# Adding expert outputs to the residual stream inside the scatter DMA instead of in a combine stage (mixer, attention and two top-2 expert layers, one Trainium2 core)

## The chip, the cores and the metric

The kernel runs on one core of a Trainium2 chip. Its metric is the device time of one execution in microseconds (us). Names used below: PE is TensorE (matrix products), DVE is VectorE, ACT is ScalarE, POOL is GpSimd, SP is SyncE, which here only issues DMAs.

## The reference

A two-layer trunk over 1040 positions (16 meta tokens and 1024 inputs) of width 1024, in fp32. Layer 0 is a state-space mixer, layer 1 windowed attention; each is followed by a mixture of experts. The part that the change touches is the end of the expert layer:

```python
def run_block(args):
    xblk, e = args
    hid = jax.nn.silu(xblk @ w_gate[e]) * (xblk @ w_up[e])
    return hid @ w_down[e]

yb = lax.map(run_block, (xb, blk_e)).reshape(n_rows, D)
contrib = yb[dest] * sgate[:, None].astype(yb.dtype)
out = jnp.zeros_like(t).at[stok].add(contrib)
...
h = h + hier_moe(rmsnorm(h, norm_ffn[layer]), ...)
```

Every token goes to two of 32 experts (`N_EXPERTS` 32, `TOP_K` 2), and the two outputs are weighted by two gates and added to the residual h. At the end of the trunk stands a last RMSNorm.

## The kernel before

The kernel has four stages one after the other: the mixer, expert layer 0 (`phase_moe(nc, t, 0)`), attention, expert layer 1 (`phase_moe(nc, t, 1, out)`). The residual h lies in SBUF the whole time, as 9 tiles of 128 tokens (the ninth has the 16 meta tokens). The order of the work on each engine is written out by hand, with semaphores between the engines.

**An expert layer.** First the router: h is normalized tile by tile, the normalized rows are stored to `xn_dram` by SP, the logits, the gates and a sorted list of rows are made. The list says for each work tile (128 slots, one expert) which token's row stands in each slot; slots beyond an expert's rows hold an index out of bounds, and the DMA leaves them out. Then comes a loop over work tiles, 32 in each layer here (64 in both). In an iteration:

- SP loads the expert's three matrices as six pieces of 1 MB into six buffers `raw` (lines 1340 to 1350). A buffer is loaded again as soon as DVE has made the low part of its old content.
- ACT casts each piece to fp32r (`hi`, line 1533), DVE subtracts to make `lo` (line 1763), PE multiplies (lines 1930 to 1932, three products for each pair of operands). `hi` and `lo` have three slots each.
- POOL gathers the 128 rows of a later work tile from `xn_dram` into `xg` (`gather`, line 1459).
- ACT copies the 128x1024 result from PSUM to `y` (`store_y`, line 1553), and POOL scatters `y` to `y_dram` (`scatter`, line 1465). `y_dram` has two rows for each token, one for each of its two experts. POOL then waits for that scatter to land before it raises `y_free`, for which the next `store_y` waits.

The order on POOL in the loop is: gather for tile e+2, wait for `y_done(e)`, scatter of tile e-1, wait for its landing:

```python
with pool.Fori(1, n_q - 2) as e:
    pool.wait_ge(xt_mm, e + 2)
    column(gi, idx_in, e + 2, e * 2 + 1)
    gather(gi[:, :])
    pool.wait_ge(y_done, e)
    scatter(e - 1, e * 2 + 2)
```

`column` copies one column of an index table and is followed by a small multiplication (lines 1450 and 1453). On ACT the eviction stands at the end of an iteration: `hi` pieces 6e+3, 6e+4, 6e+5, the cast of x, `hi` pieces of the next tile, the cast of the hidden rows, `store_y(e - 1)`. The next instruction is the `hi` cast of piece 3 of the next iteration.

**The combine.** When all scatters have landed, `y_dram` is read back, 1 MB for each tile of 128 tokens (two rows of 4 KB for each token), and DVE adds the two rows, each times its gate, to h with two `scalar_tensor_tensor` (line 1058 in layer 0, in `combine`; line 1837 in layer 1). In layer 0 (`projections`) the norm of h, its transposes and the K, V and Q products follow tile by tile, on ACT (squares, line 1028; normalize, line 1039; hi part, line 1032), DVE (line 1065) and PE (lines 1121 and 1139). In layer 1 follow squares on ACT (line 1603), two small operations on POOL (lines 1492 and 1493) that make the reciprocal root, the final scaling on DVE (line 1830) and the store to `out`.

## Time and profile before

| | |
|---|---|
| median of 3 runs | 2108.0 us (2107.89 to 2123.16) |
| time of the profiled execution | 2108.43 us |
| its span, first to last instruction | 2106.3 us |
| PE busy | 1920.0 us (91%) |
| DVE busy | 1582.0 us (75%) |
| ACT busy | 1251.5 us (59%) |
| POOL busy | 381.9 us (18%) |

"Busy" counts an instruction's own duration; waits are idle time. The profiled execution's time lies 2.1 us above its span, so sums on the span can be carried over to the time by adding that. More than half of the span is the two loops over experts, from about 450 to 1018 and from about 1484 to 2050 us.

### The profile page before, as it was taken

What the parts mean: (1) busy time and instruction counts of PE and PEld (TensorE: products, weight loads), DVE (VectorE), ACT (ScalarE), POOL (GpSimd) and SP (SyncE); (2) the same over time, 40 slices, a digit from 0 to 9 for tenths busy, and PEclk for the clock granted to TensorE, in tenths of its full rate; (3) what the DMA queues carried; (4) which work ended last, traced back from release to release, by engine and by line L of the source; (5) the groups of instructions that cost most, each with busy time, mean ns of one, the idle gap of its engine ahead of it and who ended that gap; (6) DMA issues with size and microseconds to landing.
All of it is one profiled execution on the core that took longest, in us unless ns stands there. A gap on an engine that the chain in (4) does not pass through costs nothing. (4 is left out here: it accounts for less than half of the span.)

```text
span 2106.3 us, 31639 instructions
## 1 busy us (share of the span) xinstructions
PE 1920.0 (91%) x10610; PEld 1576.8 (75%) x10610; DVE 1582.0 (75%) x1774; ACT 1251.5 (59%) x1538; POOL 381.9 (18%) x674
## 2 busy tenths in 40 slices
PE   4949999869999999999699999996999999999991
PEld 3638777758888888888598777775788888888880
DVE  8997321479999999999752376656799999999985
ACT  6615210437887777777530165544577777787771
POOL 2000000312222122221233000002122223211224
PEclk9979999989999999999899999998999999999995
DMA  4174300449999999999612110006599999999976
GB/s 105 25 76 145 110 1 1 184 153 377 385 386 378 378 381 381 385 390 389 249 61 71 35 58 2 1 1 262 205 368 364 382 383 388 398 395 395 388 300 250
DMA packets 136174, 504.72 MB, mean 240 GB/s; under 512 B 38610, under 2 KB 68626, under 8 KB 84882
## 3 DMA queue, kind: packets, MB, share of 16 engines
q1 hardware_dynamic: 114786, 468.72, 60.3%
q0 software_dynamic: 18432, 33.86, 4.2%
q10 hardware_dynamic: 2880, 1.12, 0.4%
q8 instruction: 48, 0.79, 0.2%
q14 instruction: 28, 0.23, 0.0%
HBM read 488.47 MB, written 47.32 MB: 254 GB/s over the span
## 5 line engine op out<-in xcount | busy, mean ns | idle before, releaser
L1763 DVE TENSOR_TENSOR moe_lo<-moe_raw,moe_hi 128x2048 fp32r<-128x2048 f32 x378 | 861.2, 2292 | 89.5 <-ACT moe_hi L1533 84.4
L1533 ACT CAST moe_hi<-moe_raw 128x2048 fp32r<-128x2048 f32 x374 | 712.0, 1915 | 127.1 <-PE moe_ps_g L1932 59.1
L1930 PE MATMUL moe_ps_y<-moe_hi,moe_h_hi 128*128 128x512 f32 x512 | 205.5, 401 | 3.8 <-DVE moe_h_lo L1779 3.8
L1930 PE MATMUL moe_ps_g<-moe_hi,moe_x_hi 128*128 128x512 f32 x512 | 205.9, 402 | 1.9 <-DVE moe_x_lo L1787 1.9
L1932 PE MATMUL moe_ps_y<-moe_lo,moe_h_hi 128*128 128x512 f32 x512 | 200.8, 392 | 0.0
L1931 PE MATMUL moe_ps_y<-moe_hi,moe_h_lo 128*128 128x512 f32 x512 | 200.5, 392 | 0.0
L1932 PE MATMUL moe_ps_g<-moe_lo,moe_x_hi 128*128 128x512 f32 x512 | 199.9, 390 | 0.0
L1932 PE MATMUL moe_ps_u<-moe_lo,moe_x_hi 128*128 128x512 f32 x512 | 199.7, 390 | 0.0
L1931 PE MATMUL moe_ps_g<-moe_hi,moe_x_lo 128*128 128x512 f32 x512 | 199.5, 390 | 0.0
L1930 PE MATMUL moe_ps_u<-moe_hi,moe_x_hi 128*128 128x512 f32 x512 | 199.4, 389 | 0.0
L1931 PE MATMUL moe_ps_u<-moe_hi,moe_x_lo 128*128 128x512 f32 x512 | 199.2, 389 | 0.0
L1540 ACT CAST moe_x_hi<-moe_ps_xt 128x1024 fp32r<-128x1024 f32 x60 | 61.0, 1017 | 101.3 <-PE moe_ps_xt L1915 101.3
L1930 PEld LDWEIGHTS moe_ps_y<-moe_hi,moe_h_hi 128*128 128x128 f32 x512 | 96.8, 189 | 22.5 <-DVE moe_lo L1763 4.2
L1930 PEld LDWEIGHTS moe_ps_g<-moe_hi,moe_x_hi 128*128 128x128 f32 x512 | 97.0, 189 | 20.7 <-DVE moe_x_lo L1787 2.3
L1932 PEld LDWEIGHTS moe_ps_y<-moe_lo,moe_h_hi 128*128 128x128 f32 x512 | 96.5, 189 | 20.7
L1932 PEld LDWEIGHTS moe_ps_g<-moe_lo,moe_x_hi 128*128 128x128 f32 x512 | 96.1, 188 | 21.2
L1932 PEld LDWEIGHTS moe_ps_u<-moe_lo,moe_x_hi 128*128 128x128 f32 x512 | 96.1, 188 | 20.0
L1930 PEld LDWEIGHTS moe_ps_u<-moe_hi,moe_x_hi 128*128 128x128 f32 x512 | 96.1, 188 | 19.9
L1931 PEld LDWEIGHTS moe_ps_u<-moe_hi,moe_x_lo 128*128 128x128 f32 x512 | 96.1, 188 | 19.9
L1931 PEld LDWEIGHTS moe_ps_y<-moe_hi,moe_h_lo 128*128 128x128 f32 x512 | 96.6, 189 | 18.5
L1931 PEld LDWEIGHTS moe_ps_g<-moe_hi,moe_x_lo 128*128 128x128 f32 x512 | 96.4, 188 | 18.0
L1450 POOL COPY moe_si<-moe_idx_out 128x1 int32 x64 | 50.3, 786 | 327.2 <-ACT moe_y L1553 327.2
(503 smaller groups left out, 3711.9 us busy)
## 6 DMA issues: line engine op xcount, KB each, us to landing
moe_raw<-moe_w_gate SPq DMA_DIRECT2D x128, 1024.0 KB, 8.7
moe_raw<-moe_w_up SPq DMA_DIRECT2D x128, 1024.0 KB, 9.1
moe_raw<-moe_w_down SPq DMA_DIRECT2D x128, 1024.0 KB, 8.7
mix_r<-ssm_w_glu SPq DMA_DIRECT2D x16, 512.0 KB, 6.0
xn_dram<-moe_work SPq DMA_DIRECT2D x16, 512.0 KB, 8.8
prj_yc<-y_dram SPq DMA_DIRECT2D x8, 1024.0 KB, 7.0
moe_raw<-y_dram SPq DMA_DIRECT2D x8, 1024.0 KB, 11.6
mix_r<-x SPq DMA_DIRECT2D x8, 512.0 KB, 5.1
```

The lines of the kernel that those rows point to most:

```text
L1450: G_.tensor_copy(dst[:, :], idx[:, bass.ds(tile, 1)]).then_inc(ix_step, 1)
L1533: A.copy(hi[:, slot(number, k), :], raw[:, k, :]).then_inc(hi_done, 1)
L1540: A.copy(x_hi[:, :, :].rearrange("p c m -> p (c m)"), ps_xt[:, :]).then_inc(xt_hi, 1)
L1763: V.tensor_tensor(lo[:, slot, :], raw[:, k, :], hi[:, slot, :].bitcast(F32), ALU.subtract).then_inc(lo_done, 1)
L1930: T.matmul(out, x_h, w_h, start=first, stop=False)
L1931: T.matmul(out, x_l, w_h, start=False, stop=False)
L1932: return T.matmul(out, x_h, w_l, start=False, stop=final)
```

## The change

- h is copied to DRAM (`acc_dram0`, `acc_dram1`) before the expert loop: six tiles already at the end of the stage before (mixer, attention), the others after the router's stores. These stores are issued by SP.
- The gates are stored to `gate_dram` by SP after the router, and DVE makes a table `idx_gate` that says for each slot of each work tile where its gate lies. `y_dram` and `idx_out` are gone.
- For each work tile POOL gathers 128 gates of 4 bytes from `gate_dram` into `gate` (`gather_gate`). ACT's eviction waits for that gather and multiplies by the gate on the way (`activation` with `scale=gate`).
- The scatter goes to the token's row of `acc_dram` and adds (`compute_op=ALU.add`) instead of writing to a row of its own.
- The combine is gone: after the last scatter SP loads h back, 512 KB for each tile. ACT's squares wait for the load of their tile.

```diff
+STORED = XT - 2
...
             sp.dma_start(t["gain"][:, :], t["norm_ffn"][0].partition_broadcast(P)).then_inc(gain_in, 16)
+            for i in range(STORED):
+                sp.wait_ge(h_done, (NQ - 1) * NT + i + 1)
+                sp.dma_start(t["acc_dram0"][i * P:(i + 1) * P, :], h[:, i, :]).then_inc(acc_out, 16)
             sp.wait_ge(gain_in, 16)
+            sp.wait_ge(acc_out, 16 * STORED)
...
     def project_sp(sp):
         for j in range(NT):
             i, n = TILE_ORDER[j], tile_rows(TILE_ORDER[j])
-            if j >= N_YC:
-                sp.wait_ge(h_new, 2 * (j - N_YC + 1))
-            sp.dma_start(yc[0:n, j % N_YC], y_pairs[2 * i * P:2 * (i * P + n), :].rearrange("(p k) d -> p k d", k=2)
-                         ).then_inc(yc_in[j % N_YC], 16)
+            sp.dma_start(h[0:n, i, :], t["acc_dram0"][i * P:i * P + n, :]).then_inc(h_in[j], 16)
...
         for j in range(NT):
-            combine(j)
             if j >= 2:
                 lo_part(j - 2)
...
+            for i in range(STORED, NT):
+                sp.dma_start(acc_dram[i * P:i * P + rows(i), :], h[0:rows(i), i, :]).then_inc(acc_in, 16)
             for k in range(4):
+                if k == 3:
+                    sp.wait_ge(gates_done, 1)
+                    sp.dma_start(gate_dram.rearrange("(p k) o -> p (k o)", p=P),
+                                 gates[:, :, :].rearrange("p k i -> p (k i)")).then_inc(gates_out, 16)
                 sp.wait_ge(lo_done, first_pieces(k) + 1)
                 load(k, 1)
...
             for i in range(NT if last_layer else 0):
-                if i >= NB:
-                    sp.wait_ge(h_new, 2 * (i - NB + 1))
-                sp.dma_start(yc[0:rows(i), i % NB],
-                             y_dram[2 * i * P:2 * (i * P + rows(i)), :].rearrange("(p k) d -> p k d", k=2)
-                             ).then_inc(yc_in[i % NB], 16)
+                sp.dma_start(h[:, i, :], acc_dram[i * P:(i + 1) * P, :]).then_inc(h_in[i], 16)
...
             def scatter(tile, step):
-                column(si, idx_out, tile, step)
-                G_.indirect_dma_start(y_dram[:, :], bass.IndirectOffsetOnAxis(si[:, :].bitcast(U32), 0),
-                                      y[:, :], None,
-                                      bounds_check=last_y, oob_is_err=False).then_inc(y_out, 16)
+                column(si, idx_in, tile, step)
+                G_.indirect_dma_start(acc_dram[:, :], bass.IndirectOffsetOnAxis(si[:, :].bitcast(U32), 0),
+                                      y[:, :], None, bounds_check=last_row, oob_is_err=False,
+                                      compute_op=ALU.add).then_inc(y_out, 16)
                 pool.wait_ge(y_out, tile * 16 + 16)
                 G_.tensor_tensor(unit[:, 1:2], mhalf[:, :], mhalf[:, :], ALU.mult).then_inc(y_free, 1)
+
+            def gather_gate(tile, step):
+                column(hi_gate, idx_gate, tile, step)
+                G_.indirect_dma_start(gate[:, :], None, gate_dram[:, :],
+                                      bass.IndirectOffsetOnAxis(hi_gate[:, :].bitcast(U32), 0),
+                                      bounds_check=last_gate, oob_is_err=False).then_inc(gate_in, 16)
...
+            pool.wait_ge(gate_at, 1)
+            pool.wait_ge(gates_out, 16)
+            gather_gate(0, 3)
+            pool.wait_ge(acc_in, 16 * (NT - STORED))
             with pool.Fori(1, n_q - 2) as e:
                 pool.wait_ge(xt_mm, e + 2)
-                column(gi, idx_in, e + 2, e * 2 + 1)
+                column(gi, idx_in, e + 2, e * 3 + 1)
                 gather(gi[:, :])
                 pool.wait_ge(y_done, e)
-                scatter(e - 1, e * 2 + 2)
+                scatter(e - 1, e * 3 + 2)
+                gather_gate(e, e * 3 + 3)
...
             def store_y(e, used):
                 act.wait_ge(w_used, used)
                 act.wait_ge(y_free, e + 1)
-                A.copy(y[:, :], ps_y[:, :]).then_inc(y_done, 1)
+                act.wait_ge(gate_in, e * 16 + 16)
+                A.activation(y[:, :], ps_y[:, :], ACT.Copy, scale=gate[:, 0:1]).then_inc(y_done, 1)
```

How the change moves instructions, at the two places that matter most. The first is POOL in the loop over work tiles. Before, from the copy of the scatter's index column (`moe_si`) to the end of the iteration:

```order
L1450 COPY moe_si<-moe_idx_out 128x1
L1451 REGISTER_ALU
L1453 TENSOR_TENSOR moe_unit<-moe_mhalf 128x1
L1465 DMA y_dram<-moe_y,moe_si 2080x1024
L1468 ISA
L1469 TENSOR_TENSOR moe_unit<-moe_mhalf 128x1
```

After, from the same copy on (`moe_gate` takes the gathered gates, `moe_hi_gate` the index column for them):

```order
L1449 COPY moe_si<-moe_idx_in 128x1
L1450 REGISTER_ALU
L1452 TENSOR_TENSOR moe_unit<-moe_mhalf 128x1
L1464 DMA acc_dram<-moe_y,moe_si 1040x1024
L1467 ISA
L1468 TENSOR_TENSOR moe_unit<-moe_mhalf 128x1
L1449 ISA
L1449 COPY moe_hi_gate<-moe_idx_gate 128x1
L1450 REGISTER_ALU
L1452 TENSOR_TENSOR moe_unit<-moe_mhalf 128x1
L1472 DMA moe_gate<-gate_dram,moe_hi_gate 128x1
```

The gate's gather stands behind the wait for the scatter's landing (line 1467 after, 1468 before), and ahead of the next iteration's gather of x.

The second is DVE at the end of layer 1. Before:

```order
L1779 TENSOR_TENSOR moe_h_lo<-moe_ps_ht,moe_h_hi 128x512
L1837 SCALAR_TENSOR_TENSOR h<-moe_raw,moe_gates,h 128x1024 x6
L1830 SCALAR_TENSOR_TENSOR h<-h,moe_rstd,gain 128x1024
L1837 SCALAR_TENSOR_TENSOR h<-moe_raw,moe_gates,h 128x1024 x2
L1830 SCALAR_TENSOR_TENSOR h<-h,moe_rstd,gain 128x1024
```

After:

```order
L1797 TENSOR_TENSOR moe_h_lo<-moe_ps_ht,moe_h_hi 128x512
L1848 SCALAR_TENSOR_TENSOR h<-h,moe_rstd,gain 128x1024 x8
```

The 16 additions of the combine are gone, and the 8 final scalings stand alone.

## Rows read from the trace of the kernel before

**Rows 1.** Stretches: start:end us, length, busy us (x instructions) by engine, PE clock, DMA share, GB/s.

```profile
700.00:800.00 100.00, 100.00 (x475) 83.88 (x474) 90.11 (x50) 79.12 (x58) 20.13 (x38) 1.00 0.99 380
...
2080.00:2107.00 27.00, 0.00 (x0) 0.00 (x0) 20.12 (x16) 5.75 (x10) 15.04 (x12) 0.50 0.63 249
```

**Rows 2.** Timeline of ACT, one iteration: start, us, line, operation.

```profile
1839.50 1.01 ACT L1553 COPY moe_y<-moe_ps_y 128x1024 f32<-128x1024 f32 x1
1840.43 1.92 ACT L1533 CAST moe_hi<-moe_raw 128x2048 fp32r<-128x2048 f32 x1
...
1857.24 1.02 ACT L1553 COPY moe_y<-moe_ps_y 128x1024 f32<-128x1024 f32 x1
```

**Rows 3.** Timeline of POOL, the same iteration; [idle before <-releaser].

```profile
1841.92 1.02 POOL L1465 DMA_INDIRECT y_dram<-moe_y,moe_si  x1 [0.15 <-issue]
1850.32 0.18 POOL L1469 TENSOR_TENSOR moe_unit<-moe_mhalf 128x1 f32<-128x1 f32 x1 [7.38 <-DMA y_dram<-moe_y,moe_si]
...
1851.54 1.06 POOL L1459 DMA_INDIRECT moe_xg<-xn_dram,moe_gi  x1 [0.31 <-issue]
```

**Rows 4.** Line 1465 (scatter), then line 1459 (gather): us from issue to landing.

```profile
DMA to landing us min/median/max: 3.2/8.8/9.7
...
DMA to landing us min/median/max: 3.3/8.1/11.6
```

**Rows 5.** DMA of 1520 to 1580; last number: median us to landing.

```profile
DMA packets 3816, 22.15 MB, mean 369 GB/s; under 512 B 1034, under 2 KB 1034, under 8 KB 1194
...
q0 software_dynamic: 873, 0.66, 3.3%
...
y_dram<-moe_y,moe_si POOLq DMA_INDIRECT x4, 8.6
moe_xg<-xn_dram,moe_gi POOLq DMA_INDIRECT x3, 5.7
```

**Rows 6.** The same of 1880 to 1940, where the tiles have more rows.

```profile
DMA packets 3935, 23.87 MB, mean 398 GB/s; under 512 B 707, under 2 KB 707, under 8 KB 1337
...
q0 software_dynamic: 1008, 2.58, 10.8%
...
moe_xg<-xn_dram,moe_gi POOLq DMA_INDIRECT x3, 7.6
y_dram<-moe_y,moe_si POOLq DMA_INDIRECT x3, 8.8
```

**Rows 7.** Timelines of DVE and PE: a `lo` piece, and the first product after it.

```profile
1842.38 2.29 DVE L1763 TENSOR_TENSOR moe_lo<-moe_raw,moe_hi 128x2048 fp32r<-128x2048 f32 x1 [0.34 <-ACT moe_hi L1533]
...
1845.67 0.39 PE L1930 MATMUL moe_ps_u<-moe_hi,moe_x_hi 128*128 128x512 f32 x1
```

**Rows 8.** The chain that ended last, at the end of layer 1: start, us, what.

```profile
2064.52 5.04 DMA moe_raw<-y_dram
...
2097.93 1.30 POOL moe_ss L1492
...
2099.27 0.60 POOLq L1186
2099.89 1.28 DVE h L1830
```

**Rows 9.** Timelines after layer 0: ACT's first squares; PE's transposes of two tiles.

```profile
1037.26 1.06 ACT L1028 ACTIVATE gain<-h 16x1024 f32<-16x1024 f32 x1 [10.51 <-DVE h L1058]
...
1062.22 1.16 PE L1121 MATMUL moe_ps_y<-moe_ident,prj_xn 128*128 128x128 f32 x8
...
1066.32 1.16 PE L1121 MATMUL moe_ps_xt<-moe_ident,prj_xn 128*128 128x128 f32 x8
```

**Rows 10.** Timelines of ACT and POOL at the last tile of layer 0, then of layer 1.

```profile
1025.74 1.01 ACT L1553 COPY moe_y<-moe_ps_y 128x1024 f32<-128x1024 f32 x1 [1.32 <-POOL moe_unit L1469]
...
2055.49 0.18 POOL L1469 TENSOR_TENSOR moe_unit<-moe_mhalf 128x1 f32<-128x1 f32 x1 [2.26 <-DMA y_dram<-moe_y,moe_si]
...
2059.09 1.01 ACT L1553 COPY moe_y<-moe_ps_y 128x1024 f32<-128x1024 f32 x1 [7.79 <-PE moe_ps_y L1932]
```

More of the change, by code:

```diff
@@ L1052, in project_dve @@
         V = nc.vector
-        def combine(j):
-            i, n = TILE_ORDER[j], tile_rows(TILE_ORDER[j])
-            dve.wait_ge(yc_in[j % N_YC], 16 * (j // N_YC + 1))
-            for k in range(2):
-                V.scalar_tensor_tensor(h[0:n, i, :], yc[0:n, j % N_YC, k, :], gates[0:n, k, i:i + 1],
-                                       h[0:n, i, :], ALU.mult, ALU.add).then_inc(h_new, 1)
-                dve.wait_ge(h_new, 2 * j + k + 1)
         def lo_part(j):
@@ L1181, in phase_moe @@
     h = t["h"]
-    xn_dram, y_dram = t[f"xn_dram{layer}"], t[f"y_dram{layer}"]
+    xn_dram, acc_dram, gate_dram = t[f"xn_dram{layer}"], t[f"acc_dram{layer}"], t[f"gate_dram{layer}"]
     w_gate = t["moe_w_gate"][layer].rearrange("e (p c) f -> e p c f", c=DC)
@@ L1252, in phase_moe @@
         si = sb("si", [P, 1], I32)
+        hi_gate = sb("hi_gate", [P, 1], I32)
+        gate = sb("gate", [P, 1])
         lead(nc, sb, t["qkv_at"])
@@ L1599, in _ @@
                 for i in range(NT):
[L1600 removed]
+                    act.wait_ge(h_in[i], 16)
                     if i:
@@ L1742, in _ @@
             V.scalar_tensor_tensor(idx_in[:, :], table, float(NO_ROW), row[:, :], ALU.add, ALU.min).then_inc(rows_ready, 1)
[L1743 to L1745 removed]
             link(V.tensor_tensor(after[0:1, :, :], incl[0:1, :].unsqueeze(1).to_broadcast([1, XTR, N_EXP]),
                                  iota_t[0:1, 0:XTR].unsqueeze(2).to_broadcast([1, XTR, N_EXP]), ALU.is_le))
[L1748 to L1749 removed]
+            link(V.reduce_sum(more[0:1, :], after[0:1, :, :], AX.X))
+            V.tensor_copy(tile_exp[0:1, N_EXP:TILES], more[0:1, :]).then_inc(list_ready, 1)
             V.tensor_copy(n_more[0:1, :], incl[0:1, N_EXP - 1:N_EXP]).then_inc(list_ready, 1)
@@ L1754, in _ @@
             link(V.tensor_tensor(gates[:, 0, :], col["pg"][:, :], col["tmpc"][:, :], ALU.mult))
-            link(V.tensor_tensor(gates[:, 1, :], gates[:, 0, :], col["e2"][:, :], ALU.mult))
+            V.tensor_tensor(gates[:, 1, :], gates[:, 0, :], col["e2"][:, :], ALU.mult).then_inc(gates_done, 1)
+            dve.wait_ge(rows_ready, 1)
+            V.tensor_scalar(second[:, :], table, 0.0, None, ALU.is_lt)
+            V.tensor_single_scalar(at_i[:, 0, :], idx_in[:, :], P - 1, ALU.bitwise_and)
+            link(V.tensor_single_scalar(at_i[:, 1, :], idx_in[:, :], 7, ALU.logical_shift_right))
+            link(V.tensor_copy(at[:, :, :], at_i[:, :, :]))
+            link(V.scalar_tensor_tensor(at[:, 0, :], at[:, 0, :], 2.0 * NT, at[:, 1, :], ALU.mult, ALU.add))
+            V.scalar_tensor_tensor(idx_gate[:, :], second[:, :], float(NT), at[:, 0, :], ALU.mult, ALU.add).then_inc(gate_at, 1)
             dve.wait_ge(list_ready, 2)
@@ L1833, in _ @@
             for i in range(NT if last_layer else 0):
-                n = rows(i)
-                dve.wait_ge(yc_in[i % NB], 16 * (i // NB + 1))
-                for k in range(2):
-                    V.scalar_tensor_tensor(h[0:n, i, :], yc[0:n, i % NB, k, :], gates[0:n, k, i:i + 1],
-                                           h[0:n, i, :], ALU.mult, ALU.add).then_inc(h_new, 1)
-                    dve.wait_ge(h_new, 2 * i + k + 1)
-                if last_layer and i >= 2:
-                    final_scale(i - 2)
-            if last_layer:
-                for i in range(NT - 2, NT):
-                    final_scale(i)
+                final_scale(i)
         @block.tensor
```

55 lines of the change are left out of this document (28 added, 27 removed).

## The prediction

> **What bounds the kernel now.** I read the stretches first. In a stretch inside a loop over experts PE is busy for the whole 100 us at the full clock, and the DMA engines at a share of 0.99 and 380 GB/s, while in the last 27 us PE does nothing and DVE is busy for 20.12 [rows 1]. So there are two kinds of time: two loops whose period PE sets, and two ends where the combine and the norm run. Next comes one iteration on the timelines. `store_y` starts at 1839.50 and again at 1857.24, so the period is 17.74 us [rows 2]. The waits in this stretch are short on every engine but POOL, which sits through the landing of its scatter. What counts for the change is not how busy POOL is but how its steps stand in a ring: `store_y` starts, 2.42 us later the scatter is issued (1841.92), it lands and POOL goes on at 1850.32, and the DMA after it is issued 1.22 us later, at 1851.54 [rows 2, 3]. Today this ring closes early: `y_free` comes at 1850.5 and is wanted at 1857.24. Last, the chain of waits at the end of layer 1 goes through the load of `y_dram`, DVE, POOL and DVE again to 2101.17, with 5.1 us of storing after it [rows 8].
>
> **What the ends give back.** Layer 1: the reload starts at 2064.52 in both kernels. Before, the first 1 MB took 5.04 us [rows 8]; the first 512 KB should take about 3.6 (between the 3.2 of a scatter on idle engines [rows 4] and that 5.04), so to 2068.1. Squares 1.25, then the two POOL operations and the first final scaling: about 2071.6. After that the eight tiles follow each other as POOL and DVE let them. In the trace a POOL operation beside a running DVE one takes 1.30, and the second one 0.60 with DVE idle, then DVE takes 1.28 [rows 8]. The first of the two hides under DVE's scaling of the tile before it, so a tile costs 1.28 + 0.60 + some 0.1 of handing over, 2.0. Seven more tiles end at 2085.6, and with the same 5.1 us of storing the span ends at 2090.7: 15.6 us less. That the out stores and the reload would bound it instead is unlikely: 8.4 MB in some 25 us is below the rate of the loops.
>
> Layer 0: two `scalar_tensor_tensor` go from each tile, but PE's transposes of two successive tiles stand 4.10 us apart (1062.22 and 1066.32, [rows 9]) with products of about 2.9 us and transposes of 1.2 us between, so PE takes the place of DVE as the limit. Only the front is shorter: ACT's first squares start at 1037.26, and would start at the landing of a small load, near 1034.4. I take 2.9 us. The ends together give 18.5.
>
> **What the ends lose.** The last `store_y` of a layer now waits for a gate gather that is issued 1.22 us after the scatter before it has landed, and takes at least the 3.3 us of the fastest gather [rows 4]. In layer 0 that scatter had just landed when `store_y` started at 1025.74, so it starts near 1029.9: 4.2 us. In layer 1: 2055.49 + 1.22 + 3.3 = 2060.0 in place of 2059.09, 0.9 us [rows 10]. The last two scatters of each layer also become read-and-add; priced below at 1.1 us each, 4.4 for four. So the ends net 18.5 - 5.1 - 4.4 = 9.0 us.
>
> **The loop, where the sum is decided.** Three things are new for each work tile: the scatter adds, a gather of 128 gates is issued behind the wait for the scatter's landing, and `store_y` waits for it. The ring is then: `store_y` to scatter issue 2.42, scatter landing S, its adding A, 1.22 to the gate gather's issue, its landing G, and 0.13 that I allow for an eviction that scales (the plain one takes 1.01, [rows 2]). If the ring is longer than 17.74, it is the period, whatever slack the other buffers have. S + A + G may be 17.74 - 2.42 - 1.22 - 0.13 = 13.97 us at most.
> S: the median is 8.8 [rows 4]. It hardly depends on rows: in 1520 to 1580 the software queue has 873 packets and 0.66 MB, that is 6 DMAs of about 27 rows, and a scatter lands after 8.6; in 1880 to 1940 it has 1008 packets and 2.58 MB, 7 DMAs of about 90 rows, and a scatter lands after 8.8 [rows 5, 6]. So what it costs is 128 small steps beside a queue that always has weights in it. I take 8.7.
> G: no row shows a gather of 4 bytes for each partition. From below 3.3, a gather on idle engines; from above 8.1, the median of the gathers of x [rows 4]. The nearest rows are the three gathers of about 27 rows, which leave out 101 of their 128: 5.7 [rows 5]. They also stand in the very slot where the gate gather will stand. I take 5.7.
> A: not shown either. From below 0. Between 27 and 90 rows a scatter grows by 0.2 and a gather by 1.9 [rows 5, 6]; reading 65 rows more lies between these, and I take 1.1. From above a whole further trip like a gather's, 5.7.
> Ring: 2.42 + 8.7 + 1.1 + 1.22 + 5.7 + 0.13 = 19.27, 1.53 more than now. Is that consistent? An iteration moves 6 loads of 1.05 MB, 65 rows each way and 65 more for the adding, 7.1 MB; in 19.27 us that is 368 GB/s, the load under which 5.7 and 8.6 were measured (369, [rows 5]). There are 29 such steps in each loop, so 58 x 1.53 = 88.7. The first delay of each loop is taken by slack: the `lo` piece that comes next after `store_y` on ACT and DVE ends at 1844.67 and is wanted at 1845.67 [rows 7], 1.0 us, twice: 86.7.
>
> Behind the waiting `store_y` on ACT is queued the `hi` cast of the next piece, which starts the moment the eviction ends, at 1840.43 [rows 2]; DVE waits for that, and PE for DVE. So beyond the 1.0 us the wait reaches PE in full. On POOL the gather of x for a later tile is pushed back by the gate gather, by about 2 us plus A. Issued at 1851.54 and landing 8.1 later [rows 3, 4], it is wanted by the transposes of the period after, so I take it as hidden.
>
> What the Trainium skill says of this, "DMA: Bandwidth & Descriptors", section "Anatomy of one DMA — SWDGE (gpsimd) path": a software DMA costs about 2.0 us fixed plus its bytes at 436 GB/s, so 512 bytes of gates would take 2.0, the ring would be about 15.5 and nothing would stall. The trace speaks against it in the loop (5.7 with 27 rows), and no row reaches 2.0 even idle (3.2). Of the adding, "Collectives: The Full Stack", section "The bandwidth ceiling: the fold count and why AG ≠ RS ≠ AR", says that a reduction costs twice a copy because each element has two source reads; taken for this, A would be a gather's 1.9 rather than 1.1, and the time 46 us higher. No run here shows it yet.
>
> **Edits at nothing.** The copies of h to `acc_dram`: 4.2 MB in each layer, issued while PE is in long products of the stage before, and for the last tiles behind the router's stores; their cover gone, 1 MB at 398 GB/s [rows 6] is 2.6 us in each layer. The gate table: six small DVE operations, some 1.3 us, in the time in which the first x gather is in flight; three others, 0.6 us, go from the path to the list. The gate store: 9 to 18 numbers for each partition behind loads that nobody waits for.
>
> **Sum.** 2108.4 (the profiled execution, 0.4 above the median) - 9.0 + 86.7 = 2186 us.
>
> **Rivals.**
> (1) The ring fits: G + A is at most 13.97 - 8.7 = 5.3 us, for instance G at the idle 3.3 and A up to 2.0. Then the loops keep their 17.74 us and the ends alone count: 2108.4 - 18.5 + 5.1 + 0 to 4.4, that is 2095 to 2099. For it: the gates are 512 bytes, and a 4-byte piece may pass faster than even a skipped row. Against it: landing hardly depends on bytes in [rows 5, 6]. This is the one that ends on the other side, not slower; it decides at G + A = 5.3, and up to 5.5 it would still be within 1%. To be over 1% faster it needs ends that give some 8 us more than I find.
> (2) The DMA engines become the bound rather than the ring: G is short but their share is 0.99 to 1.00 already at 380 GB/s [rows 1]. 0.27 MB more in each iteration at that rate is 0.7 us, 60 iterations: 42, less 9: 2141. Against it: 398 GB/s are moved with PE as fast as ever in [rows 6].
> (3) Adding is much dearer, A of 3 or more: ring over 21.2, 2290 and more.
>
> **How the numbers follow.** Forecast, a ring of 18.5 to 20.8: 0.53. Rival 1: 0.27, of which 0.10 over 1% faster and 0.17 within 1%. Rival 2 and short rings of 17.9 to 18.5: 0.13, of which 0.06 within 1%. Rival 3: 0.07. About 1% is what a measurement of this kernel can tell from no change. Range 2093 to 2270: from rival 1's lower end to a ring of 20.75 (G 6.6, A 1.7); it leaves out the better half of the fast cases and rival 3. Faster by over 1% 0.10, within 1% 0.24, slower 0.66.
>
> **What would show it.** In the profile after: starts of `store_y` 19.3 us apart; ACT idle before `store_y` with the gate DMA as releaser, 1 to 2 us in each iteration; PE idle before a product of `ps_u` with DVE's `lo` as releaser; gate gathers landing after 5 to 6 us, scatters after 9.8; from the last scatter's landing to the end of the span 26 us rather than 42. Wrong if `store_y` waits for nothing in the loop, or if PE's waits are on `raw` loads (then rival 2).

## The result and the profile after

The changed kernel took 2359.1 us (median of 4 runs, 2356.58 to 2361.62) against 2108.8 for the kernel before on the same chip: ratio 1.1165, 95% interval 1.1128 to 1.1202. It is 250 us slower, above the range of the prediction (2093 to 2270).

The first view is a table of stretches of the changed kernel: start:end and length in us, then busy us (number of instructions) of PE, PE's weight loads, DVE, ACT and POOL, then PE's granted clock (1.00 is 2.4 GHz, 0.50 is 1.2 GHz), the DMA share and GB/s. The first row is the stretch of [rows 1]; the others are one iteration, cut up.

```profile
700.00:800.00 100.00, 86.38 (x393) 71.49 (x393) 73.21 (x42) 64.67 (x47) 38.30 (x47) 0.93 0.87 307
...
817.00:825.00 8.00, 5.87 (x26) 4.51 (x25) 2.07 (x2) 0.29 (x1) 4.05 (x5) 1.00 0.95 365
825.00:829.00 4.00, 0.00 (x0) 0.00 (x0) 1.35 (x1) 4.00 (x3) 1.99 (x3) 0.70 0.11 35
829.00:833.00 4.00, 3.01 (x7) 2.43 (x8) 4.00 (x3) 2.70 (x3) 0.00 (x0) 0.50 0.73 155
833.00:838.00 5.00, 5.00 (x26) 4.24 (x26) 2.76 (x3) 2.46 (x2) 4.04 (x7) 0.96 0.98 336
```

PE no longer fills the loop: 86 of 100 us, with holes in which the DMA engines fall idle too (share 0.11). So neither of them is the bound. The costliest groups on the page say who waits (busy us, mean ns | idle before, releaser):

```profile
L1938 PE MATMUL moe_ps_u<-moe_hi,moe_x_hi 128*128 128x512 f32 x512 | 225.3, 440 | 195.3 <-DVE moe_lo L1781 195.3
...
L1468 POOL TENSOR_TENSOR moe_unit<-moe_mhalf 128x1 f32<-128x1 f32 x64 | 77.2, 1206 | 432.3 <-DMA acc_dram<-moe_y,moe_si 432.3
...
L1566 ACT ACTIVATE moe_y<-moe_ps_y,moe_gate 128x1024 f32<-128x1024 f32 x64 | 71.5, 1117 | 241.4 <-DMA moe_gate<-gate_dram,moe_hi_gate 241.4
```

`store_y` (line 1566) waits 241.4 us for the gate gather, in 33 of 64 tiles and not in each one, and PE loses 195.3 us of it before the products of `ps_u`. Line 1468, a product of 128 single numbers, takes 1206 ns on average; such an operation takes 0.18 alone [rows 3]. The timeline of ACT has two kinds of iteration:

```profile
798.78 1.12 ACT L1566 ACTIVATE moe_y<-moe_ps_y,moe_gate 128x1024 f32<-128x1024 f32 x1
...
824.71 1.11 ACT L1566 ACTIVATE moe_y<-moe_ps_y,moe_gate 128x1024 f32<-128x1024 f32 x1 [8.08 <-DMA moe_gate<-gate_dram,moe_hi_gate]
...
843.29 1.12 ACT L1566 ACTIVATE moe_y<-moe_ps_y,moe_gate 128x1024 f32<-128x1024 f32 x1
```

One step of 25.9 us, then one of 18.6; over 58 steps of both loops (the first 29 of each) the mean is 22.15 against 17.75 before, and 28 of them are longer than 22. 58 x 4.40 is 255 us, and the spans differ by 252.9: the loops hold the whole loss, and all else together gives back about 2 us. The timeline of POOL in the long step shows where its 25.9 us go:

```profile
801.19 1.64 POOL L1464 DMA_INDIRECT acc_dram<-moe_y,moe_si  x1 [0.15 <-issue]
812.19 1.78 POOL L1468 TENSOR_TENSOR moe_unit<-moe_mhalf 128x1 f32<-128x1 f32 x1 [9.36 <-DMA acc_dram<-moe_y,moe_si]
813.91 2.25 POOL L1449 COPY moe_hi_gate<-moe_idx_gate 128x1 int32 x1
816.24 2.29 POOL L1452 TENSOR_TENSOR moe_unit<-moe_mhalf 128x1 f32<-128x1 f32 x1
818.67 1.09 POOL L1472 DMA_INDIRECT moe_gate<-gate_dram,moe_hi_gate  x1
...
833.19 1.21 POOL L1468 TENSOR_TENSOR moe_unit<-moe_mhalf 128x1 f32<-128x1 f32 x1 [4.78 <-DMA acc_dram<-moe_y,moe_si]
```

2.4 to the scatter's issue, 11.0 to POOL's next operation, 6.5 from there to the gate gather's issue, 6.0 to `store_y`. The 6.5 us are three tiny operations, which end at 813.97, 816.16 and 818.53. DVE's timeline has this beside them:

```profile
811.62 6.85 DVE L1781 TENSOR_TENSOR moe_lo<-moe_raw,moe_hi 128x2048 fp32r<-128x2048 f32 x3
```

Three subtractions without a gap, ending near 813.9, 816.2 and 818.4: each POOL operation ends when a subtraction ends. The Trainium skill, "SBUF — State Buffer", section "Who interferes with whom", says that a DVE instruction with two SBUF inputs contends with a GpSimd instruction that reads SBUF, and the page's section "Summary: rules for kernel authors" that the second of the two to issue fully blocks until the first finishes. The `lo` subtraction has two (`raw` and `hi`), and the trace agrees, at 2.25 and 2.29 us for operations that take 0.2 alone. The rest of this trace says the same: 153 small POOL operations begin while a `lo` subtraction runs, and take 1.71 us in the median and up to 2.31; 51 begin while DVE runs one of its subtractions or products with one input in PSUM (`x_lo`, `h_lo`, `hid`), and take 0.18 to 0.20.

Before the change, the same run of three subtractions stands at the same phase, and POOL is done just ahead of it (timelines of POOL and DVE, kernel before; `store_y` had started at 611.55):

```profile
622.84 0.19 POOL L1469 TENSOR_TENSOR moe_unit<-moe_mhalf 128x1 f32<-128x1 f32 x1 [7.84 <-DMA y_dram<-moe_y,moe_si]
623.29 0.18 POOL L1450 COPY moe_gi<-moe_idx_in 128x1 int32 x1 [0.27 <-issue]
623.56 0.19 POOL L1453 TENSOR_TENSOR moe_unit<-moe_mhalf 128x1 f32<-128x1 f32 x1
```
```profile
624.39 6.86 DVE L1763 TENSOR_TENSOR moe_lo<-moe_raw,moe_hi 128x2048 fp32r<-128x2048 f32 x3
```

The run lies from 12.8 to 19.7 us after `store_y`. A landing at 11.3 gets its three operations through in 0.9 us. A landing at 13.4 does not get the gate gather out before the run is over, at 19.9. That is a step, not a slope. The kernel before came to this edge once: in the step whose `store_y` starts at 1732.98 the landing comes 12.2 us after it, the run starts at 1745.81, and the third of POOL's operations and the issue behind it are held up (POOL's timeline; the x gather goes out 3.2 us after the landing instead of 1.2):

```profile
1745.86 2.29 POOL L1453 TENSOR_TENSOR moe_unit<-moe_mhalf 128x1 f32<-128x1 f32 x1
1748.30 2.93 POOL L1459 DMA_INDIRECT moe_xg<-xn_dram,moe_gi  x1
```

Last, the stall costs PE's clock. Its timeline around the hole, with the first product after it at twice the usual length:

```profile
829.99 0.80 PE L1938 MATMUL moe_ps_u<-moe_hi,moe_x_hi 128*128 128x512 f32 x1 [7.12 <-DVE moe_lo L1781]
...
833.15 0.53 PE L1939 MATMUL moe_ps_u<-moe_hi,moe_x_lo 128*128 128x512 f32 x1
833.52 0.40 PE L1940 MATMUL moe_ps_u<-moe_lo,moe_x_hi 128*128 128x512 f32 x1
```

After 7.1 us of idleness PE runs at 1.2 GHz until about 833.2. The eight products that start from 829.99 on take 3.5 us to pass instead of 1.8, so 1.7 us more. The pair of steps adds up: 25.9 + 18.6 - 2 x 17.74 = 9.0, of which 7.1 is idleness and 1.7 the clock.

### The profile page after: what moved, and what is told of

Same layout as the page of the kernel before. It is cut to its first block and busy times, and to the rows that moved or that the text cites. A ratio compares the mean times of both kernels' runs of the same rounds, so it can differ in the third digit from the quotient of the medians.

```text
span 2359.2 us, 31996 instructions
## 1 busy us (share of the span) xinstructions
PE 1983.7 (84%) x10610; PEld 1615.3 (68%) x10610; DVE 1535.8 (65%) x1746; ACT 1251.3 (53%) x1538; POOL 671.2 (28%) x866
## 5 line engine op out<-in xcount | busy, mean ns | idle before, releaser
L1938 PE MATMUL moe_ps_u<-moe_hi,moe_x_hi 128*128 128x512 f32 x512 | 225.3, 440 | 195.3 <-DVE moe_lo L1781 195.3
L1938 PEld LDWEIGHTS moe_ps_u<-moe_hi,moe_x_hi 128*128 128x128 f32 x512 | 108.5, 212 | 230.0 <-DVE moe_lo L1781 207.1
L1939 PE MATMUL moe_ps_u<-moe_hi,moe_x_lo 128*128 128x512 f32 x512 | 218.2, 426 | 0.0
L1940 PE MATMUL moe_ps_u<-moe_lo,moe_x_hi 128*128 128x512 f32 x512 | 216.3, 423 | 0.0
L1468 POOL TENSOR_TENSOR moe_unit<-moe_mhalf 128x1 f32<-128x1 f32 x64 | 77.2, 1206 | 432.3 <-DMA acc_dram<-moe_y,moe_si 432.3
L1566 ACT ACTIVATE moe_y<-moe_ps_y,moe_gate 128x1024 f32<-128x1024 f32 x64 | 71.5, 1117 | 241.4 <-DMA moe_gate<-gate_dram,moe_hi_gate 241.4
L1786 DVE TENSOR_TENSOR moe_x_lo<-moe_ps_xt,moe_x_hi 128x1024 fp32r<-128x1024 f32 x60 | 73.5, 1224 | 81.6 <-ACT moe_x_hi L1552 81.6
L1449 POOL COPY moe_si<-moe_idx_in 128x1 int32 x64 | 27.3, 427 | 346.2 <-ACT moe_y L1566 346.1
L1939 PEld LDWEIGHTS moe_ps_u<-moe_hi,moe_x_lo 128*128 128x128 f32 x512 | 109.0, 213 | 22.6
L1464 POOL DMA_INDIRECT acc_dram<-moe_y,moe_si x64 | 107.2, 1674 | 15.4 <-issue 15.4
```

What stands on the lines that cost most here:

```text
L1449: G_.tensor_copy(dst[:, :], idx[:, bass.ds(tile, 1)]).then_inc(ix_step, 1)
L1464: G_.indirect_dma_start(acc_dram[:, :], bass.IndirectOffsetOnAxis(si[:, :].bitcast(U32), 0), y[:, :], None, bounds_check=last_row, oob_is_ ...
L1468: G_.tensor_tensor(unit[:, 1:2], mhalf[:, :], mhalf[:, :], ALU.mult).then_inc(y_free, 1)
L1566: A.activation(y[:, :], ps_y[:, :], ACT.Copy, scale=gate[:, 0:1]).then_inc(y_done, 1)
L1786: V.tensor_tensor(x_lo[:, :, :].rearrange("p c m -> p (c m)"), ps_xt[:, :], x_hi[:, :, :].bitcast(F32).rearrange("p c m -> p (c m)"), ALU. ...
L1938: T.matmul(out, x_h, w_h, start=first, stop=False)
```

## The experiments

The first four kernels ran together on one chip (before: 2110.0 us), the next four together (2108.7), the next three (2110.7), the last by itself (2109.9). `landed` below is the second half of `scatter`: the wait for `y_out` and the operation that raises `y_free`. The times after `store_y` that follow are differences of start times in the timelines of ACT and POOL.

**1. Gate gather first** (`e1_gate_first`). Two calls change places, with their step numbers:

```diff
-                scatter(e - 1, e * 3 + 2)
-                gather_gate(e, e * 3 + 3)
+                gather_gate(e, e * 3 + 2)
+                scatter(e - 1, e * 3 + 3)
```

> Only the order on POOL changes: the gather of the gates for tile e is issued before the scatter of tile e-1 instead of behind its landing, so gather and scatter run side by side. Theory (the ring store_y, scatter landing, gate gather, store_y sets the period of 22.2 us): the ring is then 2.4 + some 2 for issuing the gates + 6.4 to 11 for the scatter, under 17.74, PE sets the period again and the 4.5 us on each of 60 steps go: 2359 - 267, about 2092, a little under the kernel before. Rival A (the added DMA work, 0.27 MB of reading and 144 small packets for each tile, fills the DMA engines and sets the period): waits on the weight loads appear and the time stays above 2150. Rival B (scatter 11 us and more under full load, with 2 us of gate issue ahead of it, is itself too long): ACT waits for POOL's y_free, and the time is 2100 to 2130.

Measured: 2251.4 us (ratio 1.067, 1.065 to 1.069). The gate waits are gone and 108 us with them, but 141 remain. The wait is the one that rival B named, ACT for `y_free`, but rival B had 2100 to 2130 us. POOL's timeline shows the ring:

```profile
799.06 1.05 POOL L1472 DMA_INDIRECT moe_gate<-gate_dram,moe_hi_gate  x1
800.12 1.65 POOL L1449 COPY moe_si<-moe_idx_in 128x1 int32 x1
801.86 2.13 POOL L1452 TENSOR_TENSOR moe_unit<-moe_mhalf 128x1 f32<-128x1 f32 x1
804.14 3.50 POOL L1464 DMA_INDIRECT acc_dram<-moe_y,moe_si  x1 [0.15 <-issue]
815.52 1.58 POOL L1468 TENSOR_TENSOR moe_unit<-moe_mhalf 128x1 f32<-128x1 f32 x1 [7.88 <-DMA acc_dram<-moe_y,moe_si]
```

What stood ahead of the scatter put it among the next subtractions of DVE: issued 7.6 us after `store_y` instead of 2.4, landed some 18 to 21 after it, and `store_y` waits for `y_free` (166.2 us in all, 59 times), every 20.4 us. The issue of the scatter itself is stretched, 3.50 us against 1.63.

**2. No gates** (`e2_no_gate`). Leaves out the gates.

```diff
-                gather_gate(e, e * 3 + 3)
...
-                act.wait_ge(gate_in, e * 16 + 16)
-                A.activation(y[:, :], ps_y[:, :], ACT.Copy, scale=gate[:, 0:1]).then_inc(y_done, 1)
+                A.copy(y[:, :], ps_y[:, :]).then_inc(y_done, 1)
```

> The gather of gates is left out and the eviction is the plain copy, so the output lacks the gates; the adding scatter stays. Theory (ring through the gate gather): without its last link the ring is 2.4 + 11 at most, and the loops go back to 17.74 us a tile: 2090 to 2100. Rival A (the adding scatter's DMA work sets the period): above 2130, with waits on the loads.

Measured: 2203.9 us (1.044, 1.041 to 1.047). The expectation fell, and with it the theory that the gate ring is all. The waits of 600 to 1000 (us in total, times, longest) name another ring:

```profile
POOL moe_unit L1468 <- DMA acc_dram<-moe_y,moe_si: 188.4, 21, 10.0
...
PEld moe_ps_xt L1918 <- DMA moe_xg<-xn_dram,moe_gi: 33.8, 16, 2.8
```

PE's transposes wait for the gather of x. POOL issues that gather only behind its wait for the scatter's landing: landed 13.3 after `store_y`, three operations held up by DVE, x gather issued at 19.9, landed some 8.7 later, so 28.6, where ACT's cast of the transposed x starts at 17.8 + 10.0 if nothing delays it. That is the step with which each such series begins. In most of the others the late x gather holds up the scatter too, which is issued 5.65 after `store_y` instead of 2.42 and lands at 15 to 18, with the next x gather at about 22. No wait for `raw` appears. The prediction took this gather as hidden.

**3. Scatter without adding** (`e3_plain_scatter`). Leaves out the sum: rows are written instead of added.

```diff
-                                      compute_op=ALU.add).then_inc(y_out, 16)
+                                      ).then_inc(y_out, 16)
```

> The scatter writes the row instead of adding it, so the output lacks the sum; gates and everything else stay. Theory (each link of the ring counts, and the adding is about 2 to 3 us of it): the scatter lands after 8.8 again, the hand-over stays short because it falls where it fell before, the ring is 2.4 + 8.8 + 1.2 + 6 = 18.4, and the time is about 2140. Rival (what costs is the three POOL operations that queue behind DVE, adding or not): every other step stays at 25 us and the time stays above 2280.

Measured: 2259.0 us, one run. Between the two theories. The plain scatter lands at 11.5 rather than 13.4 and often gets through ahead of DVE's run; then the step is 17.8. Long steps are still as long (mean 26.1), but 15 of 58 instead of 28. In 14 of the 15 the scatter itself is issued late, 3.2 to 5.5 after `store_y`, behind an x gather that POOL got out only 17.5 us after the `store_y` before. So the adding acts by the number of long steps, not by a length added to each.

**4. Gate index copied ahead** (`e4_gate_prep`). The column copy of the gate gather and the operation behind it are moved in front of the scatter, so one of three operations stays between the landing and the gate gather's issue (`fetch_gate`, without its index copy):

```diff
-            def scatter(tile, step):
+            def scatter(tile, step, gate_of=None):
+                if gate_of is not None:
+                    column(hi_gate, idx_gate, gate_of, step)
+                    step = step + 1
                 column(si, idx_in, tile, step)
...
+                if gate_of is not None:
+                    fetch_gate()
...
-                scatter(e - 1, e * 3 + 2)
-                gather_gate(e, e * 3 + 3)
+                scatter(e - 1, e * 3 + 2, e)
```

> The index column for the gate gather is copied before the scatter, so that behind the scatter's landing only one small POOL operation stands ahead of the gate gather instead of three. Theory (POOL's small operations each wait for a running DVE lo subtraction, which makes the hand-over 6.5 us in every other step): the hand-over falls to about 2 us in the long steps, 4.5 us on 30 steps, about 2220. Rival (the hand-over is long for another reason, a late semaphore or the DMA's landing): no change, 2359.

Measured: 2308.9 us, one run: 50 less than the changed kernel, 90 more than expected. In the typical long step the gate gather is issued 15.3 after `store_y` instead of 19.9, but the scatter later, at 3.0, and the issue is now what is held up (POOL's timeline, 3.13 against 1.05 to 1.09 us alone):

```profile
801.15 0.18 POOL L1471 TENSOR_TENSOR moe_unit<-moe_mhalf 128x1 f32<-128x1 f32 x1 [8.01 <-DMA acc_dram<-moe_y,moe_si]
801.49 3.13 POOL L1480 DMA_INDIRECT moe_gate<-gate_dram,moe_hi_gate  x1 [0.15 <-issue]
```

The new theory: all of the loss but the DMA engines' part comes from POOL being serial. It has a blocking wait for a landing in the middle, and what is queued behind that wait (gate gather, x gather) comes out late, later still for DVE's subtractions. Four kernels test it.

**5. No gates, no adding** (`e5_no_gate_plain`): edits 2 and 3 together. Leaves out the gates and the sum.

> Leaves out the gates and the sum: y is evicted without a scale, no gate is gathered, and the scatter writes its rows instead of adding them. What is left of the change is the early stores of h and the short reload. Theory (serial POOL: what lengthens a tile is the adding scatter's later landing and the operations queued behind it): scatter issued 2.4 us after each store_y, landed by 11.5, x gather issued by 13, store_y 17.8 us apart as before, and the savings of the two tails stay: 2085 to 2095 us. Rival (part of the loss of the gateless kernel, 2204 us, comes from the moved stores of h or the changed DRAM tensors and not from adding): over 2110 us with periods over 17.9.

Measured: 2088.5 us (0.990, 0.988 to 0.992), every step 17.8. Without the sum layer 1 gets other values and so other lists of rows, but the kernel before has the right ones and 17.8 in every step too. So the early stores of h, the short reload and the new tables cost nothing in the loop, and the ends give 20 us.

**6. No gates, x gather before the landing wait** (`e6_no_gate_x_early`). Leaves out the gates; adds.

```diff
-                pool.wait_ge(xt_mm, e + 2)
-                column(gi, idx_in, e + 2, e * 3 + 1)
-                gather(gi[:, :])
                 pool.wait_ge(y_done, e)
-                scatter(e - 1, e * 3 + 2)
-                gather_gate(e, e * 3 + 3)
+                scatter(e - 1, e * 2 + 2)
+                pool.wait_ge(xt_mm, e + 3)
+                column(gi, idx_in, e + 3, e * 2 + 3)
+                gather(gi[:, :])
+                landed(e - 1)
```

Before the loop one more x gather is issued, and `scatter` here ends with its issue.

> Leaves out the gates; the scatter adds. As the gateless kernel of 2204 us, but POOL issues the x gather of the tile after next before it waits for the scatter's landing, not behind it. Theory (the second ring: landing 13.5 to 16.7 us after store_y, three POOL operations, x gather 8.7 us, transposes): the x gather is out by some 14 us after store_y instead of 20 to 22, PE's transposes no longer wait for it, periods return to 17.8 us, total 2090 to 2105 us. Rival (the adding itself takes DMA engine time that the loads need, or its landing is late for store_y however POOL is ordered): over 2150 us, with ACT waiting for the unit operation behind the landing or the casts for raw loads.

Measured: 2139.6 us (1.015, 1.013 to 1.017). The x ring is gone: 64 us less than experiment 2 and no wait of the transposes. But it is neither the 2090 to 2105 of the theory nor over 2150. The waits of 600 to 1000 are now those for the weights:

```profile
ACT moe_hi L1548 <- DMA moe_raw<-moe_w_gate: 31.6, 21, 1.7
...
ACT moe_hi L1548 <- DMA moe_raw<-moe_w_up: 20.8, 25, 1.2
...
ACT moe_hi L1548 <- DMA moe_raw<-moe_w_down: 12.1, 22, 0.8
```

Of each loop's first 29 steps, 4 in layer 0 and 13 in layer 1 take 17.8 us, the others 18.2 to 19.3. Layer 1's first tiles have few rows: POOL's queue takes 5.5% of the DMA engines over its first seven steps (1545 to 1669), and 13.9% from 1790 to 2060. So the steps lengthen where the tiles have more rows. That the weights loaded ahead carry the first steps besides is likely, not shown. The DMA queues of the same stretch, experiment 5 and then experiment 6 (packets, MB, share of 16 engines):

```profile
DMA packets 25966, 153.56 MB, mean 384 GB/s; under 512 B 5804, under 2 KB 5804, under 8 KB 8644
...
q0 software_dynamic: 6480, 11.65, 7.6%
```
```profile
DMA packets 24493, 144.58 MB, mean 361 GB/s; under 512 B 5518, under 2 KB 5518, under 8 KB 8176
...
q0 software_dynamic: 6135, 10.91, 10.7%
```

For the same 0.5 MB in each iteration, as the profile counts them, POOL's queue takes more engine time, 10.7% against 7.6%; the bytes of an iteration, 6.8 MB, now need 18.8 us. This is the bound of the prediction's second rival, beneath two rings that hid it.

**7. Gate gather before the landing wait, x gather behind it** (`e7_gate_before_landing`). Computes all.

```diff
                 scatter(e - 1, e * 3 + 2)
                 gather_gate(e, e * 3 + 3)
+                landed(e - 1)
```

> Computes all. As the changed kernel, but the gate gather is issued right behind the scatter's issue and before POOL waits for its landing; the x gather stays behind that wait. Theory (two rings, the gate's goes and the x gather's stays): scatter out at 2.4 us, gate out by 9, no wait of store_y for its gate, and periods as those of the gateless kernel or a little longer, since the two extra POOL operations delay nothing else: 2200 to 2230 us. Rival (the gate gather is harmful by its place between DVE's subtractions wherever it stands): as the kernel with the gate first, 2250 us or more.

Measured: 2194.4 us (1.040, 1.035 to 1.044), just below the theory's 2200. One wait for a gate is left in the whole kernel, of 4.8 us; the transposes wait for x as in experiment 2 (34.6 us, 19 times, between 600 and 1000), mean step 19.44. The theory's ring of x carries both kernels.

**8. All three issued before the wait** (`e8_both_early`). Computes all. Index columns of scatter and gate gather are copied one tile ahead, behind the landing.

```diff
+                pool.wait_ge(y_done, e)
+                pace()
+                scatter()                      # issue only
+                gather_gate()
+                pool.wait_ge(xt_mm, e + 3)
+                column(gi, idx_in, e + 3, e * 3 + 4)
                 gather(gi[:, :])
+                landed(e - 1)
+                column(si, idx_in, e, e * 3 + 5)
+                pool.wait_ge(gate_in, e * 16 + 16)
+                column(hi_gate, idx_gate, e + 1, e * 3 + 6)
```

`pace` is a small operation like the one in `column`.

> Computes all. The index columns of the scatter and of the gate gather are copied one tile ahead; when y is ready POOL issues scatter, gate gather and the x gather of the tile after next, and only then waits for the scatter's landing. Theory (all of the loss is serial waiting on POOL): scatter out at about 2.6 us after store_y, x gather by 13, no wait of store_y for a gate and none of PE for x, periods 17.8 to 18.0 us, total 2090 to 2110 us, so at or below the kernel before. Rival (DMA engines are the bound with 3 indirect transfers in flight beside the loads, as the prediction's second rival had it, 2141 us): periods over 18.3 us with ACT or DVE waiting for raw loads.

Measured: 2141.8 us (1.016, 1.013 to 1.018). The same work as the changed kernel, in another order on POOL, 217 us faster, and still 33 slower than before. The rival was right: the waits are those for `raw`, as in experiment 6.

**9. The same with a plain scatter** (`e9_both_early_plain`). Leaves out the sum.

> Leaves out the sum: the kernel with scatter, gate gather and x gather all issued before the landing wait (2141.8 us), but the scatter writes its rows instead of adding them; gates are gathered and used. Theory (of the 53 us between that kernel and the gateless one with plain scatters, 2088.5 us, all is DMA engine time of the adding, and gates in the right place cost nothing): periods 17.8 us, no waits for raw loads, 2088 to 2094 us. Rival (part of it is the gate gathers and the third transfer in flight): 2105 us or more, with ACT waiting for raw loads.

Measured: 2090.5 us (0.990, 0.988 to 0.992), no wait for `raw`. With 8 this is the price of adding once no ring is closed: 51 us. With 5 it is the price of the gates in the right place: 2 us, as between 6 and 8. That is no more than the 2.0 us by which the kernel before differs between the runs of 5 and of 9.

**10. Gate gather behind the landing, x gather before it** (`e10_gate_behind_x_early`). Computes all; the loop of 6 with `gather_gate(e, ...)` behind `landed(e - 1)`.

> Computes all. As the changed kernel (2359 us), with the gate gather behind the scatter's landing as there, but the x gather issued before the landing wait, so that only the ring through the gate is left. Theory (the changed kernel's time is the gate ring alone, x gather is no part of it there): store_y still waits for the gate, long steps of 25 to 26 us beside short ones, 2320 to 2370 us. Rival (the x gather, queued on POOL behind the gate gather, is what puts POOL's next operations beside DVE's subtractions, and without it the ring would close in the 19 to 20 us that the prediction computed): 2180 to 2230 us.

Measured: 2335.2 us (1.106, 1.104 to 1.109), long steps mostly of 25.0 to 26.4. The gate ring alone makes all but 24 us of the changed kernel's loss.

**11. Half of one weight piece not loaded** (`e11_half_load`). Experiment 6 with 0.5 MB less in each iteration. Leaves out the gates and half of a piece of each expert's last matrix.

```diff
+                    if kk == 5:
+                        dst, src = dst[:, 0:FW // 2, :], src[:, 0:FW // 2, :]
```

> Leaves out the gates and, of each expert's last of six weight pieces, half of the load (the other half of the buffer keeps old numbers), so that an iteration moves 0.5 MB less of some 6.8 MB; all else is as in the gateless kernel with the x gather early (2139.6 us, periods 18.8 us, adding scatter). Theory (that kernel is bound by the DMA engines): 0.5 MB less at 361 GB/s is 1.4 us, more than the 1.1 us by which it is over 17.8, so periods return to 17.8 us, no waits for raw loads, 2088 to 2098 us. Rival (the adding scatter delays single pieces by blocking a queue, whatever the bytes): over 2120 us.

Measured: 2097.0 us (0.994, 0.992 to 0.996), no waits for `raw`. The DMA engines were the bound of 6 and 8, and fewer bytes lift it. Here the DMA share of 700 to 800 is 0.96 at 351 GB/s; in [rows 1] it was 0.99 at 380 with nobody waiting. So that share doesn't tell how near the bound is.

**12. The gate ring with a short hand-over** (`e12_short_hand_over`). Experiment 8 with `gather_gate()` moved behind `landed(e - 1)`. Against experiment 10 two things differ: one operation stands between landing and issue in place of three, and the scatter's index column is copied ahead as well. Computes all.

> Computes all. The gate gather stands behind the scatter's landing as in the changed kernel, but its index column is already copied and the x gather is issued before the landing wait, so that one small POOL operation stands between landing and the gate gather's issue instead of three. Theory (POOL operations behind the landing each end only when the DVE subtraction beside them ends, 6.5 us for three, where the prediction had 1.22): the long steps lose 2 to 5 us, hand-over at most 2.3, ring about 2.2 + 10.8 + 0.2 to 2.3 + 6.0 + 0.1 = 19.3 to 21.4 us, total 2200 to 2300 us. Rival (the landing times of scatter and gate gather make the long steps, not the operations between): within 30 us of the kernel with three operations there, 2335 us.

Measured: 2246.9 us (1.065, 1.059 to 1.070); the profiled execution, 2222.5, was the fastest of its four. 88 us less than experiment 10. POOL's timeline, with `store_y` at 760.44 and 779.46:

```profile
761.98 1.63 POOL L1466 DMA_INDIRECT acc_dram<-moe_y,moe_si  x1
...
770.56 1.08 POOL L1458 DMA_INDIRECT moe_xg<-xn_dram,moe_gi  x1 [0.16 <-issue]
771.67 0.20 POOL L1472 TENSOR_TENSOR moe_unit<-moe_mhalf 128x1 f32<-128x1 f32 x1
772.03 1.04 POOL L1475 DMA_INDIRECT moe_gate<-gate_dram,moe_hi_gate  x1 [0.15 <-issue]
```

Most steps are 18.5 to 20 us: 1.5 to the issue, 9.7 to POOL's operation behind the landing, 0.4, 7.4 for the gate. The scatter had landed before 771.67, for POOL comes to that operation straight from the x gather's issue, without a wait. The length is that of the ring which the prediction computed, 19.27, with other parts. 10 of 58 steps, in which landing or issue meets DVE's run, are 24.4 us on average.

The scatter is issued 1.5 us after `store_y` in most steps here, and 2.1 or 2.4 in experiment 10, whose long steps have POOL's next operation at 12.2 to 14.6, around the edge at 12.8; here it is at 11.2 to 11.7 in about half of the steps. So part of the 88 us can be the earlier scatter and not the two operations, and no run divides them. Experiment 4 took the same two operations away with the scatter 0.5 us later than in the changed kernel, and gained 50.

Put in a row, from the bottom up: before 2109; without adding and gates 2088 (the ends, -20); adding, nothing else in a ring 2140 (+51); gates in the right place 2142 (+2); gate gather behind the landing with one operation between 2247 (+105); with three, and the scatter issued later, 2335 (+88); x gather behind it too 2359 (+24). No version that computes all beats the kernel before: the adding costs 51 and the ends give 20. Of the 51, 44 lie in the two loops, from the first `store_y` to the last (1122.3 us in experiment 6, 1078.3 in 5). The rest is mostly the last scatter of each layer, which nothing hides: POOL's next operation comes 6.1 and 6.4 us after its issue (experiment 6) instead of 3.3.

## Why the prediction was wrong

The sign, the mechanism and its place in the profile were right: `store_y` waits for the gate with ACT idle, PE waits before `ps_u` on DVE's `lo`, rival 1 didn't happen. Experiment 8 shows that this order on POOL costs 217 of the 250 us. The size was off by 173 us, and these are the steps.

- **The hand-over of 1.22 us, the step that failed.** It was read from [rows 3], where POOL passes ahead of DVE's run of subtractions. Moved by the adding to 13.4 us after `store_y`, the same kind of operations took 6.5. The prediction added durations as if they didn't depend on when they happen. It had the effect in its own rows: at the end of layer 1 it reads 1.30 us for a POOL operation beside a running DVE one. Experiment 4 (two operations fewer, the scatter a little later) gained 50 us; experiment 12 against 10 (two fewer, the scatter earlier) 88.
- **"Starts of `store_y` 19.3 us apart".** A uniform ring was wrong in kind. In a long step the buffers `raw` are all in use (SP issues no load from 818.8 until 829.97, when DVE's next `lo` has ended), the DMA engines fall idle (share 0.11 from 825 to 829), and the next scatter takes 6.4 us instead of 11.0, so a step of 18.6 follows. The mean is 22.15. "If the ring is longer than 17.74, it is the period" holds only where no term of it depends on the step before.
- **A, the adding, 1.1 us, mis-sized.** By the landings, 10.6 us in experiment 2 against 8.8 in 5: 1.8, of which 0.6 is a longer issue (1.61 against 1.03 us). On idle engines it is over 3: 6.6 (2327.11 to 2333.73) against the 3.2 of [rows 4]. The rule on reductions that the prediction cites from the Trainium skill ("Collectives: The Full Stack", section "The bandwidth ceiling: the fold count and why AG ≠ RS ≠ AR") gave 1.9, and the trace is nearer to that, though the 0.6 of issue is none of that rule's. What was missing is what it brings about: 2 us more move the landing over the edge of DVE's run.
- **S of 8.7 and G of 5.7** held: plain scatters land in 8.8 (experiment 5); gate gathers have a median of 6.1 in the changed kernel, and `store_y` starts 6.0 after the issue in the step shown. But the DMA engines move 307 GB/s there; in experiment 12 the median is 7.1. The short form of a gather was a fair stand-in for 512 bytes; the 2.0 us that the prediction takes from the Trainium skill ("DMA: Bandwidth & Descriptors", section "Anatomy of one DMA — SWDGE (gpsimd) path") was not.
- **"I take it as hidden", the gather of x**, was wrong in mechanism, small in effect here: 24 us (experiments 10 against the changed kernel), since the gate ring was longer. Without that ring it is the bound: 64 us (2 against 6).
- **PE's clock** stood in no term. At 1.7 us for each of 28 long steps it is some 48 us, an estimate from the one stall shown.
- **Rival 2** gave 2141, and experiment 8 measured 2141.8. Its parts are near too: 42 us for the loops where the 58 steps cost 45 (mean 18.53 against 17.75), and 9 given back by the rest where it was 10 to 12. But its reason, 0.27 MB more in each iteration at 380 GB/s, isn't what the profile shows: the counted bytes stay, the rate falls from 384 to 361 GB/s, and 17 of 58 steps stay at 17.8 in experiment 6. So that it comes within 1 us is luck. And it stood as an alternative to the ring; it is a floor under it.
- **The ends.** Layer 1: from the last landing (2333.73) to the end of the span (2359.2) 25.5 us, where 26 was predicted instead of 42. The rows below (timelines of ACT and DVE) show the final scalings 2.0 us apart, as computed. The last `store_y` waits for its gate in both layers; its step grew by 6.0 and 2.6 us, not 4.2 and 0.9. Layer 0: PE's last transposes start 49.5 us after the last `store_y` before and 46.8 in the changed kernel, a dearer last scatter included; PE was not quite the limit that the prediction took it for, since they now stand 3.8 us apart instead of 4.1. Together everything outside the 58 steps gave 2 us where 9.0 were predicted.

```profile
2325.05 1.11 ACT L1566 ACTIVATE moe_y<-moe_ps_y,moe_gate 128x1024 f32<-128x1024 f32 x1 [10.31 <-DMA moe_gate<-gate_dram,moe_hi_gate]
2337.36 1.06 ACT L1616 ACTIVATE moe_xg<-h 128x1024 f32<-128x1024 f32 x1 [11.19 <-DMA h<-acc_dram]
```
```profile
2339.56 1.28 DVE L1848 SCALAR_TENSOR_TENSOR h<-h,moe_rstd,gain 128x1024 f32<-128x1024 f32 x1 [25.51 <-POOL moe_rstd L1505]
2341.56 1.29 DVE L1848 SCALAR_TENSOR_TENSOR h<-h,moe_rstd,gain 128x1024 f32<-128x1024 f32 x1 [0.72 <-POOL moe_rstd L1505]
```

- **Edits at nothing** were right: experiment 5, which has them all, keeps 17.8 in every step.
- **The range** begins at 2093, "rival 1's lower end", where rival 1's own sum gives 2095. Nothing hangs on it.

What stays open: how large PE's clock loss is in stalls of other lengths, whether the time that the adding takes on the DMA engines goes by rows or by bytes, and how the 88 us between experiments 10 and 12 divide; none of these was tried.

## What to carry to other kernels

Before a step is put behind a blocking wait on an engine, ask of everything queued behind that wait when it must be out, and issue what doesn't depend on the wait ahead of it: the same work in another order on POOL was 217 us faster. A duration holds for the phase in which it was read; if a change moves an operation by 2 us, look at what runs beside its new place, above all a small POOL operation next to DVE instructions with two inputs in SBUF. And a ring that no longer fits hides the bounds beneath it, so each must be priced alone before one concludes that removing the ring pays.

## What was unexpected of the hardware

- A POOL operation on 128 numbers took 0.18 to 2.29 us according to what DVE did beside it, and so did the issue of an indirect DMA: 1.05 to 3.16 us for the gate gather in the changed kernel, 3.50 in the median for the 59 adding scatters that experiment 1 issued beside a `lo` subtraction, against 1.63 in the changed kernel. "SBUF — State Buffer" of the Trainium skill, section "Who interferes with whom", infers that generating descriptors isn't held up by a `tensor_tensor`; the issues here were, and an indirect DMA has its indices in SBUF.
- The adding scatter landed after 10.6 us against 8.8 for a plain one under load, and took 10.7% of the DMA engines against 7.6% for the same 0.5 MB per iteration (experiments 2, 5 and 6).
- A DMA share of 0.99 was seen with slack (kernel before) and without (experiment 6); the wait for `raw`, or its absence, told them apart.
